# A transformer block on one core: diagonal blocks of a triangular inverse laid out one per partition, keys and queries left unnormalised, attention outputs handled four query tiles at a time

## The chip, the core and the metric

The kernel runs on one core of a Trainium2 chip. The metric is the device time of one execution in microseconds. Three runs of the kernel before took 1466.9 to 1472.14 us; their median is 1470.46 us.

## What is computed

One residual block over 1024 tokens of width 1024: a norm, one projection, two kinds of attention heads, an output projection, and a feed-forward part. The change lies in the heads, of which there are eight forgetting-attention heads ("fox", width 64) and four gated delta-rule heads ("gdn", width 128). Cut to what matters:

```python
# fox head: softmax over the causal prefix with a decay bias, then an RMS norm of the output
logits = q @ k.T * scale + cum[:, None] - cum[None, :]        # masked
o = softmax(logits) @ v;  o = rms_norm(o, fox_out_norm)
# gdn head: q and k are first divided by their norms (rsqrt(sum(x*x) + EPS))
m = strict_lower((k * beta) @ k.T * decay)
t_inv = inverse(eye + m)                                      # unit lower triangular
u = t_inv @ (v * beta);  w = t_inv @ (k * beta * exp(gc))
a = (q @ k.T) * decay
# then a scan over the chunks of tokens
v_new = u_c - w_c @ state
o_c = (q * exp(gc)) @ state + a_c @ v_new
state = state * g_last + k_dec.T @ v_new
```

The kernel uses chunks of 128 tokens (the reference has 64), which is the same function.

## The kernel before

The program has four stages on TensorE: the input projection (`in_up`), the heads, the output projection (L2970 to L2972), and the feed-forward part (`up` and `d_product`). The change is in the heads.

In the heads stage three kinds of work are woven together: the **preparation** of a gdn head, the **scan** over the chunks of the gdn head before it, and the **fox tiles**, 64 of them (8 heads of 8 query tiles). The preparation of head `p` is a list of steps, `HEAD_PREP`. Each step is a *fill*: TensorE writes four 128x128 results into one of three PSUM banks, and VectorE or ScalarE reads the bank (`read`). A fill is either four transposes (`four_turned`, L2722) or four products in float32 (`four_products`, L2717). A name such as `("X", 0, 4)` is step, half of the head (four of its eight chunks) and level. `k`, `q`, `v`, `z` turn the loaded rows; `knT`, `qnT`, `kbT`, `qdT` turn scaled copies back; `N` and `A` are the two score products. The inverse is built by doubling: from blocks of 1 to blocks of 128 in seven levels. Level 0 is `M0`; each level above it is a product `X` (masked on its way out), a product `TX`, and a transposed copy `XR` (a product at the last level). `W` and `U` apply the inverse.

The norm of k and of q goes around four engines: ScalarE squares the bank (`square`), VectorE sums and adds EPS (`norm_mean`), GpSimd raises to the power -0.5 (`norm_power`, L2430), and VectorE scales (`norm_scale`, L1990). Only then can `knT` or `qnT` be turned.

A fox tile is: `scores` on TensorE (L2828 to L2830), a masked row maximum on VectorE (`fox_scores`), the exponential on ScalarE, `turn` (L2846), a copy by VectorE or ScalarE in turn, and `times_v` (the `pv` items, L2860) into a PSUM bank. Then ScalarE copies the 64 output columns out (L1513) and squares them with a sum (L1516), once per tile. After four tiles VectorE forms the mean square (`mean`, L2081 and L2083), GpSimd takes the power (L2485), and VectorE scales the four tiles one at a time (`fox_norm`, L2091).

The order on every engine is fixed when the program is built. `plan_prep`, `plan_scan` and `plan_fox` give each item an engine and a planned time, and `ORDER` is each engine's list sorted by it; the constant `PHASE` is the planned length of a head. An engine takes its list in order: whatever it waits for holds everything behind it. All loads and stores are issued by SyncE, also in a planned order.

## Time and profile before

| | us |
|---|---|
| median of three runs | 1470.46 |
| span of the profiled execution, first to last instruction | 1465.4 |
| TensorE busy in the span | 1379.2 (94%) |
| VectorE, ScalarE, GpSimd busy | 944.7, 658.4, 573.6 |
| heads stage, from the first turn of k in the first head to the end of the last `pv` | 313.3 to 718.4 |

The median lies 5 us above the span; the start and the end of the program lie outside the span. A busy time is the union of an engine's instructions. Matmuls overlap their neighbours, so the time that a matmul costs in a sequence is the distance from its start to the next start, not its listed duration.

### The profile page before, as it was taken

How to read it: one execution, taken by the hardware profiler on the slowest of the kernel's cores; microseconds unless marked ns; L12 is line 12 of the kernel's file. 1: busy time of each engine (PE TensorE's matmuls, PEld its weight loads, DVE VectorE, ACT ScalarE, POOL GpSimd, SP SyncE). 2: the span in 40 equal slices, each digit the busy share in tenths (PEclk: the TensorE clock that was granted, in tenths of full speed). 3: DMA queues.
4: the chain of work that ended last, by engine and by line, in shares of the span. 5: the costliest groups of instructions: out<-in, count | busy, mean ns of one | idle time of the engine just before them, and what ended most of it. 6: DMA issues, size and time to landing. Idle time of an engine off the chain costs nothing.

```text
span 1465.4 us, 20680 instructions
## 1 busy us (share of the span) xinstructions
PE 1379.2 (94%) x7379; PEld 1165.7 (80%) x7379; DVE 944.7 (64%) x1506; ACT 658.4 (45%) x1404; POOL 573.6 (39%) x470
## 2 busy tenths in 40 slices
PE   5999999998989899898899889999999999999997
PEld 4778888877989899797688768888888778888885
DVE  6977777765567665765545799655655584444557
ACT  6654334435455555555433532333233344445453
POOL 3733322314152441614401377665564164442001
PEclk9999999998999999999999999999999999999999
DMA  7143333245113131013222244444442995333533
GB/s 207 47 129 103 115 115 115 88 151 179 30 59 102 49 97 44 16 44 102 87 73 86 85 125 159 158 158 159 158 158 102 329 320 168 94 99 105 202 98 144
DMA packets 135325, 177.88 MB, mean 121 GB/s; under 512 B 10492, under 2 KB 82732, under 8 KB 135224
## 3 DMA queue, kind: packets, MB, share of 16 engines
q1 hardware_dynamic: 135224, 176.56, 37.5%
q8 instruction: 60, 0.98, 0.3%
q14 instruction: 41, 0.34, 0.1%
HBM read 124.05 MB, written 52.48 MB: 120 GB/s over the span
## 4 chain that ended last, share of the span: by engine, by line
PE 76%; DVE 10%; issue 5%; POOL 4%; ACT 2%; DMA 2%; SPq 1%; DVEq 0%; POOLq 0%; ACTq 0%
PE ps L2717 7%; PE ps L3018 7%; PE ps L3020 7%; PE ps L3019 7%; PE ps L3031 6%; PE ps L3032 6%; PE ps L3033 6%; PE ps L2668 5%; PE ps L2670 5%; PE ps L2669 5%; PE ps L2860 3%; PE ps L2970 2%; PE ps L2972 2%; PE ps L2971 2%; PE ps L2722 2%
## 5 line engine op out<-in xcount | busy, mean ns | idle before, releaser
L3031 PE MATMUL ps<-db_hi,da_hi 128*128 128x512 f32 x448 | 175.3, 391 | 4.1 <-DVE db_lo L2288 4.0
L3032 PE MATMUL ps<-db_lo,da_hi 128*128 128x512 f32 x448 | 174.4, 389 | 0.0
L3033 PE MATMUL ps<-db_hi,da_lo 128*128 128x512 f32 x448 | 174.3, 389 | 0.0
L2286 DVE TENSOR_TENSOR da_lo<-a_raw,da_hi 128x512 fp32r<-128x512 f32 x112 | 85.6, 764 | 121.3 <-ACT da_hi L1756 121.2
L1756 ACT ACTIVATE da_hi<-a_raw 128x512 fp32r<-128x512 f32 x112 | 70.7, 631 | 159.3 <-PE ps L3033 136.9
L3018 PE MATMUL ps<-bt_hi,ring_hi 128*128 128x512 f32 x320 | 127.2, 397 | 5.3 <-DVE ring_lo L2208 5.2
L3020 PE MATMUL ps<-bt_hi,ring_lo 128*128 128x512 f32 x320 | 126.0, 394 | 0.0
L3019 PE MATMUL ps<-bt_lo,ring_hi 128*128 128x512 f32 x320 | 125.4, 392 | 0.0
L2668 PE MATMUL ps<-i_bt_hi,i_ring_hi 128*128 128x512 f32 x280 | 111.0, 396 | 3.2 <-DVE i_ring_lo L1848 1.8
L2670 PE MATMUL ps<-i_bt_hi,i_ring_lo 128*128 128x512 f32 x280 | 110.3, 394 | 0.0
L2669 PE MATMUL ps<-i_bt_lo,i_ring_hi 128*128 128x512 f32 x280 | 110.0, 393 | 0.0
L3031 PEld LDWEIGHTS ps<-db_hi,da_hi 128*128 128x128 f32 x448 | 84.1, 188 | 25.3 <-DVE db_lo L2288 7.9
L3033 PEld LDWEIGHTS ps<-db_hi,da_lo 128*128 128x128 f32 x448 | 84.1, 188 | 17.4
L3032 PEld LDWEIGHTS ps<-db_lo,da_hi 128*128 128x128 f32 x448 | 84.1, 188 | 17.1
L2534 POOL TENSOR_TENSOR o_rs<-o_ms,halves 128x1 f32<-128x1 f32 x24 | 16.5, 687 | 203.7 <-DVE o_ms L2186 92.3
L2477 POOL TENSOR_TENSOR q_lo<-q,q_hi 128x128 fp32r<-128x128 f32 x64 | 30.6, 479 | 165.1 <-ACT q_hi L1492 156.8
L1655 ACT ACTIVATE ring_hi<-s_w 128x512 fp32r<-128x512 f32 x64 | 40.3, 632 | 120.5 <-PE ps L3020 116.8
L2860 PE MATMUL ps<-v_tok,probs_t 128*128 128x64 f32 x576 | 78.1, 273 | 14.8 <-DVE probs_t L2039 12.7
L2288 DVE TENSOR_TENSOR db_lo<-wd,db_hi 128x512 fp32r<-128x512 f32 x112 | 88.7, 792 | 0.0
L2860 PEld LDWEIGHTS ps<-v_tok,probs_t 128*128 128x128 f32 x576 | 72.5, 193 | 19.3 <-DVE probs_t L2039 15.2
L3018 PEld LDWEIGHTS ps<-bt_hi,ring_hi 128*128 128x128 f32 x320 | 60.7, 190 | 18.8 <-DVE ring_lo L2208 5.6
L3020 PEld LDWEIGHTS ps<-bt_hi,ring_lo 128*128 128x128 f32 x320 | 60.5, 189 | 14.2
(367 smaller groups left out, 3655.2 us busy)
## 6 DMA issues: line engine op xcount, KB each, us to landing
a_raw<-act_dram SPq DMA_DIRECT2D x112, 256.0 KB, 2.6
act_dram<-s_act SPq DMA_DIRECT2D x64, 256.0 KB, 2.2
wd<-in_w_down_dram SPq DMA_DIRECT2D x15, 1024.0 KB, 7.7
act_dram<-c SPq DMA_DIRECT2D x48, 256.0 KB, 4.8
w_top<-in_w_up_dram SPq DMA_DIRECT2D x18, 512.0 KB, 4.3
w_bot<-in_w_up_dram SPq DMA_DIRECT2D x16, 512.0 KB, 5.5
i_top<-in_w_in_dram SPq DMA_DIRECT2D x14, 512.0 KB, 4.0
i_bot<-in_w_in_dram SPq DMA_DIRECT2D x14, 512.0 KB, 5.3
```

Of the source, the lines that this page charges most:

```text
L2288: nc.vector.tensor_tensor(db_lo[s][:, :], d_moving(n), db_hi[s][:, :].bitcast(F32), ALU.subtract).then_inc(d_lo_ready, 1)
L2668: nc.tensor.matmul(acc, i_ring_hi[r][:, k, :], b_hi[:, k, :], start=(first and k == 0), stop=False, skip_group_check=True)
L2669: nc.tensor.matmul(acc, i_ring_hi[r][:, k, :], b_lo[:, k, :], start=False, stop=False, skip_group_check=True)
L2670: last = nc.tensor.matmul(acc, i_ring_lo[r][:, k, :], b_hi[:, k, :], start=False, stop=(k == HK - 1), skip_group_check=True)
L2717: last = nc.tensor.matmul(bank(f)[:, i * P:(i + 1) * P], lhs(i), rhs(i), start=True, stop=True)
L2860: last = nc.tensor.matmul(fox_o(i)[:, 0:FOX_DIM], probs_t[n % 2][:, kb - 4 * c, :], v_tok[h % 2][:, kb, hh * FOX_DIM:(hh + 1) * FOX_DIM], ...
L3018: nc.tensor.matmul(acc, ring_hi[r][:, k, :], b_hi[:, k, :], start=(first and k == 0), stop=False, skip_group_check=True)
L3019: nc.tensor.matmul(acc, ring_hi[r][:, k, :], b_lo[:, k, :], start=False, stop=False, skip_group_check=True)
L3020: last = nc.tensor.matmul(acc, ring_lo[r][:, k, :], b_hi[:, k, :], start=False, stop=(k == HK - 1), skip_group_check=True)
L3031: nc.tensor.matmul(acc, da_hi[s][:, cols], db_hi[s][:, :], start=start, stop=False, skip_group_check=True)
L3032: nc.tensor.matmul(acc, da_hi[s][:, cols], db_lo[s][:, :], start=False, stop=False, skip_group_check=True)
L3033: return nc.tensor.matmul(acc, da_lo[s][:, cols], db_hi[s][:, :], start=False, stop=stop, skip_group_check=True)
```

## The change

The change takes levels 0 to 3 of the inverse out of the fills. The 16x16 diagonal blocks of `N` (8 blocks in each of 8 chunks, 64 in all) are written by eight small DMAs to DRAM and read back with one block in each of 64 partitions. VectorE inverts them there with 16 instructions on 64 partitions (`lanes`), the result goes to DRAM, and eight small DMAs put the blocks on the diagonal of `t_low`, from which level 4 starts. `HEAD_PREP` shrinks: the steps `kbT`, `qnT`, `qdT`, `M0`, `X` and `TX` of levels 1 to 3, `XR` of levels 1 and 2 and one mask turn are gone, and six empty places stand ahead of the first `X`. In all 250 fills become 153: 49 turned fills and 48 product fills fewer.

The scales are moved. `kn` is now k times beta over its square sum (reciprocal and product on VectorE, no power), `N` and `A` use k and q as loaded, the root of the sum goes into `vb`, `exp(gc)` for q is one exponential (`g_last_out`) and one GpSimd product (`q_grown`), and q's norm enters through EPS in the output norm.

Fox outputs: the eight tiles of a head share one PSUM bank, 64 columns each. ScalarE copies four tiles at once and squares them in place in PSUM; VectorE sums the squares; two VectorE products scale four tiles. The first `pv` of each group of four waits for `tail_mean` of the group before it; in the kernel before each `pv` waited for the output copy of the tile before in the same bank. `PHASE` goes from 90 to 68.

```diff
 HEAD_PREP = [
+    ("k", 0, 0), ("k", 1, 0), ("q", 0, 0), ("knT", 0, 0), ("q", 1, 0), ("knT", 1, 0), ("N", 0, 0), ("N", 1, 0),
+    ("v", 0, 0), ("A", 0, 0), ("v", 1, 0), ("A", 1, 0), ("z", 0, 0), ("z", 1, 0), None, None, None, None, None, None,
+    ("X", 0, 4), ("XR", 0, 3), ("X", 1, 4), ("XR", 1, 3), ("TX", 0, 4), ("TX", 1, 4),
...
+            def load_lanes(p):
+                for g in range(2):
+                    sp.wait_ge(dve_prep, DVE_PREP[("read", (p, "N", g, 0))])
+                for b in range(NBLOCK):
+                    rows = slice(BLOCK * b, BLOCK * (b + 1))
+                    sp.dma_start(n_dram[NT * b:NT * (b + 1), :, :].rearrange("t k c -> k t c"),
+                                 n_low[rows, :, :, rows].rearrange("k g t c -> k (g t) c")).then_inc(lanes_moved, 16)
+                sp.wait_ge(lanes_moved, lane_moves(p, "blocks"))
+                sp.dma_start(lane_n[0:LANES, :], n_dram.rearrange("l k c -> l (k c)")).then_inc(lanes_moved, 16)
+            def store_lanes(p):
+                sp.wait_ge(lane_step, LANE_OPS * (p + 1))
+                sp.dma_start(t_dram.rearrange("l c k -> l (c k)"), lane_t[0:LANES, :]).then_inc(lanes_moved, 16)
+                sp.wait_ge(lanes_moved, lane_moves(p, "out"))
...
+                for b in range(NBLOCK):
+                    rows = slice(BLOCK * b, BLOCK * (b + 1))
+                    sp.dma_start(t_low[rows, :, :, rows].rearrange("c g t k -> c (g t) k"),
+                                 t_dram[NT * b:NT * (b + 1), :, :].rearrange("t c k -> c t k")).then_inc(lanes_moved, 16)
...
             def norm_scale(name):
+                nc.vector.reciprocal(k_scale[:, g, :], means[:, g, :]).then_inc(scale_step, 1)
...
+                nc.vector.tensor_tensor(k_scale[:, g, :], k_scale[:, g, :], gates_all[:, BETA, p, four], ALU.mult).then_inc(scale_step, 1)
...
+                nc.vector.tensor_tensor(kn[:, g, :, :], bank4(FILL[name] - 1), wide(k_scale[:, g, :], P), ALU.mult).then_inc(dve_prep, 1)
...
+            def lanes(p, part):
...
+                elif part == 2:
+                    dve.wait_ge(lane_step, done + 12)
+                    nc.vector.tensor_tensor(lane(lane_p, 0, (64, 8), (8, 8), (1, 8)), lane(lane_n, 8, (1, 8), (0, 8), (16, 8)),
+                                            lane(lane_t, 0, (0, 8), (1, 8), (16, 8)), ALU.mult).then_inc(lane_step, 1)
+                    dve.wait_ge(lane_step, done + 13)
+                    nc.vector.tensor_reduce(lane(lane_x, 0, (1, 64)), lane(lane_p, 0, (8, 64), (1, 8)), AX_X, ALU.add).then_inc(lane_step, 1)
...
             def fox_out(i):
-                nc.scalar.activation(mixed_fox(qb // HT, h)[:, qb % HT, hh * FOX_DIM:(hh + 1) * FOX_DIM], fox_o(i)[:, 0:FOX_DIM], ACT.Copy)
-                if i >= 1:
-                    act.wait_ge(fox_read, i)
-                nc.scalar.activation(sq_fox[:, :], fox_o(i)[:, 0:FOX_DIM], ACT.Square, accum_out=fox_ss[:, hh, qb:qb + 1]).then_inc(fox_read, 1)
+                nc.scalar.activation(mixed_fox(half, h)[:, :, hh * FOX_DIM:(hh + 1) * FOX_DIM], fox_o4(i // NT, half), ACT.Copy).then_inc(fox_copied, 1)
+                act.wait_ge(fox_copied, i // HT + 1)
+                nc.scalar.activation(fox_o4(i // NT, half), fox_o4(i // NT, half), ACT.Square).then_inc(fox_read, 1)
...
             def mean(tail):
+                dve.wait_ge(fox_read, 2 * n + half + 1)
+                nc.vector.tensor_reduce(fox_ss[:, n % 2, cols], fox_o4(n, half), AX_X, ALU.add).then_inc(rr_ready, 1)
...
             def fox_norm(n, half):
+                nc.vector.tensor_tensor(o, o, wide(fox_ms[:, n % 2, half * HT:(half + 1) * HT], FOX_DIM), ALU.mult).then_inc(fox_scaled, 1)
+                dve.wait_ge(fox_scaled, FOX_NORM[("fox", (n, half))])
+                nc.vector.tensor_tensor(o, o, stacked(fox_norm_row[:, :], HT), ALU.mult).then_inc(mixed_ready, 1)
...
             def prep(name):
                 elif what == "X":
+                    if lev == BASE:
+                        pe.wait_ge(lanes_moved, lane_moves(p, "t_low"))
...
             def times_v(i, c):
                 if c == 0:
-                    if OUT_BEFORE[i] is not None:
-                        pe.wait_ge(fox_read, OUT_BEFORE[i] + 1)
+                    if i >= HT and qb % HT == 0:
+                        pe.wait_ge(tail_mean, MEAN[("fox", (i - HT) // NT, 1 - qb // HT)])
```

The first place is TensorE at the start of the third gdn head, from the first turn of k (`c_raw_k`) on. Other names: `probs` and `probs_t` belong to fox tiles, `u_all`, `a_t`, `kd` to the scan. Before:

```order
L2722 MATMUL ps<-const,c_raw_k 128x128 x4
L2846 MATMUL ps<-const,probs_161 128x128 x3
L2722 MATMUL ps<-const,c_raw_v 128x128 x4
L2860 MATMUL ps<-v_tok_139,probs_t_163 128x64 x3
L2722 MATMUL ps<-const,c_raw_q 128x128 x4
L2898 MATMUL ps<-u_all_151,a_t_147 128x128
L2901 MATMUL ps<-u_all_151,kd_143 128x128
L2722 MATMUL ps<-const,c_raw_v 128x128 x4
```

After:

```order
L2838 MATMUL ps<-const,c_raw_k 128x128 x4
L2953 MATMUL ps<-const,probs_166 128x128 x3
L2838 MATMUL ps<-const,c_raw_k 128x128 x4
L2965 MATMUL ps<-v_tok_144,probs_t_168 128x64 x3
L2838 MATMUL ps<-const,c_raw_q 128x128 x4
L3004 MATMUL ps<-u_all_156,a_t_152 128x128
L3007 MATMUL ps<-u_all_156,kd_148 128x128
L2935 MATMUL ps<-k_split_163,q_hi_170 128x512
L2936 MATMUL ps<-k_split_163,q_lo_172 128x512
```

Both halves of k are now turned ahead of q and v.

The second place is VectorE in the same head, with the instructions on the lanes (`lane_n`, `lane_p`, `lane_t`, `lane_x`) and what stands among them after the change; none of the lane rows stands in the kernel before:

```order
L2152 TENSOR_TENSOR a_t_151<-ps,decay 128x512
L2088 COPY lane_t<-lane_n 64x8
L2090 TENSOR_TENSOR lane_p<-lane_n,lane_t 64x8
L2092 COPY lane_t<-lane_n 64x4x2
L2094 TENSOR_TENSOR lane_t<-lane_p,lane_n 64x4x2
L2097 TENSOR_TENSOR lane_p<-lane_t 64x8
L2100 TENSOR_TENSOR lane_t<-lane_t,lane_p 64x4x2
L2184 TENSOR_TENSOR v_new<-u_all_156,ps 128x128
L2105 TENSOR_TENSOR lane_p<-lane_n,lane_t 64x64 x2
L2108 TENSOR_REDUCE lane_x<-lane_p 64x32
L2111 TENSOR_TENSOR lane_p<-lane_t,lane_x 64x64 x2
L2114 TENSOR_REDUCE lane_t<-lane_p 64x2x4x4
```

The scan's `v_new` and `state` and a fox copy now stand in VectorE's list behind instructions that wait for DMAs.

The third place is TensorE in the same head where `times_v` goes from the fourth to the fifth fox head (`v_tok_144` to `v_tok_143`). Before:

```order
L2860 MATMUL ps<-v_tok_139,probs_t_163 128x64 x4
L2722 MATMUL ps<-const,t_inv 128x128 x4
L2828 MATMUL ps<-k_split_157,q_hi_166 128x256
L2829 MATMUL ps<-k_split_157,q_lo_168 128x256
L2830 MATMUL ps<-causal_bf,ident_bf 128x128
L2860 MATMUL ps<-v_tok_139,probs_t_164 128x64 x4
L2846 MATMUL ps<-const,probs_161 128x128
L2717 MATMUL ps<-t_inv,n_low 128x128 x4
L2717 MATMUL ps<-xb,r_inv 128x128 x4
L2860 MATMUL ps<-v_tok_138,probs_t_163 128x64
```

After:

```order
L2965 MATMUL ps<-v_tok_144,probs_t_168 128x64 x4
L2833 MATMUL ps<-t_low,n_low 128x128 x4
L2935 MATMUL ps<-k_split_162,q_hi_171 128x256
L2936 MATMUL ps<-k_split_162,q_lo_173 128x256
L2937 MATMUL ps<-causal_bf,ident_bf 128x128
L2953 MATMUL ps<-const,probs_166 128x128
L2965 MATMUL ps<-v_tok_144,probs_t_169 128x64 x4
L2838 MATMUL ps<-const,t_low 128x128 x4
L2965 MATMUL ps<-v_tok_143,probs_t_168 128x64
```

Two product fills and a turn between the last `pv` of one fox head and the first of the next have become one turned fill.

## Rows read from the trace of the kernel before

**Rows 1.** The page: busy time of each engine; the chain that ended last, by engine.
```profile
PE 1379.2 (94%) x7379; PEld 1165.7 (80%) x7379; DVE 944.7 (64%) x1506; ACT 658.4 (45%) x1404; POOL 573.6 (39%) x470
...
PE 76%; DVE 10%; issue 5%; POOL 4%; ACT 2%; DMA 2%; SPq 1%; DVEq 0%; POOLq 0%; ACTq 0%
```

**Rows 2.** Windows: four heads and the tail; stretch, length, busy by engine, PEclk, DMA.
```profile
313.27:406.80 93.53, 81.95 (x617) 74.77 (x615) 58.27 (x129) 45.37 (x135) 27.54 (x32) 0.93 0.32 102
406.80:495.78 88.98, 81.82 (x684) 77.15 (x682) 57.56 (x143) 48.99 (x159) 32.08 (x35) 0.98 0.25 72
495.78:583.89 88.11, 81.47 (x677) 76.72 (x676) 58.91 (x142) 47.82 (x150) 31.03 (x34) 0.98 0.25 73
583.89:674.31 90.42, 81.10 (x667) 76.24 (x666) 58.58 (x152) 48.21 (x158) 32.60 (x37) 0.98 0.09 25
674.31:718.41 44.10, 36.25 (x266) 31.47 (x265) 28.30 (x75) 30.39 (x99) 28.86 (x22) 0.96 0.40 108
```

**Rows 3.** Groups of TensorE by shape: the X products and the XR turns.
```profile
L2717 PE MATMUL ps<-t_inv,n_low 128*128 128x128 f32 x384 | 51.3, 278 | 0.0
...
L2722 PE MATMUL ps<-const,t_inv 128*128 128x128 f32 x160 | 23.8, 273 | 0.0
```

**Rows 4.** Timeline of TensorE, third head: start, duration, line, count of records.
```profile
521.32 1.00 PE L2860 MATMUL ps<-v_tok,probs_t 128*128 128x64 f32 x8
522.16 0.61 PE L2722 MATMUL ps<-const,qn 128*128 128x128 f32 x4
522.60 0.39 PE L2875 MATMUL ps<-state,w_all 128*128 128x128 f32 x2
...
538.71 1.06 PE L2717 MATMUL ps<-t_inv,n_low 128*128 128x128 f32 x8
539.60 1.06 PE L2717 MATMUL ps<-xb,r_inv 128*128 128x128 f32 x8
```

**Rows 5.** Waits of TensorE from 305 to 722 us: total, times, longest.
```profile
PE ps L2860 <- DVE probs_t L2039: 12.7, 11, 2.6
PE ps L2722 <- DVE qn L1990: 8.9, 8, 2.3
PE ps L2722 <- DVE kn L1990: 5.9, 5, 1.7
```

**Rows 6.** Groups of GpSimd in the heads: busy, mean ns, idle before.
```profile
L2430 POOL TENSOR_TENSOR powers<-means,minus_half 128x4 f32<-128x4 f32 x16 | 16.6, 1039 | 30.1 <-DVE means L1983 30.0
```

**Rows 7.** Groups of VectorE and ScalarE in the heads, same columns.
```profile
L2027 DVE TENSOR_TENSOR t_inv<-t_inv,ps 128x512 f32<-128x512 f32 x40 | 27.5, 687 | 27.1 <-PE ps L2717 26.9
L2056 DVE TENSOR_TENSOR v_new<-u_all,ps 128x128 f32<-128x128 f32 x28 | 7.9, 282 | 6.7 <-PE ps L2875 6.7
L1981 DVE TENSOR_REDUCE sums<-qn 128x4 f32<-128x512 f32 x8 | 5.5, 683 | 1.4 <-ACT qn L1451 1.3
L2083 DVE TENSOR_TENSOR fox_ms<-fox_ss,fox_rr 128x4 f32<-128x4 f32 x16 | 3.0, 189 | 0.6
...
L1473 ACT ACTIVATE r_inv<-ps 128x512 f32<-128x512 f32 x40 | 23.8, 594 | 23.0 <-PE ps L2722 22.6
L1527 ACT ACTIVATE mixed_half<-ps 128x128 f32<-128x128 f32 x32 | 8.8, 274 | 20.1 <-DVE state L2067 16.6 <-PE ps L2898 2.5 <-DVE state L2064 1.1
```

**Rows 8.** DMA issues: count, KB each, median us to landing.
```profile
act_dram<-s_act SPq DMA_DIRECT2D x64, 256.0 KB, 2.2
c_raw_k<-proj_dram SPq DMA_DIRECT2D x3, 512.0 KB, 3.4
```

**Rows 9.** Timeline of SyncE's queue near the start: start, duration of the issue.
```profile
12.86 2.65 SPq L986 DMA_DIRECT2D gate_w<-in_w_in_dram  x1
...
20.38 0.29 SPq L996 DMA_DIRECT2D row_bias<-in_gdn_dt_bias_dram  x1
20.72 0.31 SPq L997 DMA_DIRECT2D row_a<-in_gdn_a_log_dram  x1
```

**Rows 10.** A window in the fourth head, with the columns of rows 2.
```profile
610.00:615.00 5.00, 5.00 (x31) 4.87 (x31) 1.39 (x5) 1.02 (x4) 1.80 (x2) 0.69 0.28 79
```

## What the trace of the kernel before lets one predict

> **What bounds the kernel now.** I read the page first, then windows, groups of instructions, waits, and the timeline. The page says that TensorE is busy for 94% of the span and makes up 76% of the chain that ended last [rows 1]. The change lies in the heads alone, so the windows count. In them TensorE is busy 81 to 82 us of each head's 88 to 94, and 36 of the 44 us of the tail; VectorE works 58 to 59 us per head, ScalarE 45 to 49, GpSimd 28 to 33 [rows 2]. So TensorE's own work bounds the heads, with some 7 to 12 us of idle per head. Its waits name two things: at the start of a head it waits for the scaled k and q (`kn` 5.9 us, `qn` 8.9 us in all), and `pv` waits for VectorE's copies, 12.7 us in 11 waits [rows 5]. The first kind goes back to GpSimd's power, 1039 ns for four columns and 30 us of waiting for the sums before it [rows 6]; VectorE stands still behind it, which also holds copies.
>
> **The price of a fill.** Listed durations overlap, so I take starts. Two product fills start at 538.71 and 539.60: 0.89 us for four products (eight records, since a float32 product makes two). A turned fill takes from 522.16 to 522.60: 0.44 us. Eight records of `pv` take from 521.32 to 522.16: 0.84 us [rows 4]. The count is checked by the groups: 384 records of X are 48 fills, 160 records of turned `t_inv` are 40 [rows 3].
>
> **1. Fills taken out: -64.3 us.** 48 product fills (X and TX of levels 1 to 3) at 0.89 are 42.7 us; 49 turned ones at 0.44 are 21.6 us. All of it is on the engine that bounds the stage, 16 us of each head's 81.
>
> **2. The trip of the blocks: +27 us.** This is new: between the last `N` and the first `X` the blocks go to DRAM, to VectorE's lanes, to DRAM, and back, and nothing of the head but `v`, `A` and `z` can be done meanwhile. Step by step:
> - VectorE's read of `N`: 0.69 us [rows 7] and a signal, 0.8.
> - Eight small stores. An issue on an idle queue comes 0.34 us after the one before (20.38, 20.72) [rows 9], so the last starts after 2.4. For the landing the nearest row is the smallest transfer with one, 256 KB in 2.2 us; a load of 512 KB takes 3.4 [rows 8]. 8 KB should be no slower than 256: 2.2. Together 4.6.
> - The load with one block per partition: 2.2.
> - 16 VectorE instructions. Six with 8 elements at 0.19, four with 64 and two sums over 128 at 0.28 (the 128x128 form), two products of 512 at 0.69 and two sums of 512 at 0.68 [rows 7]: 1.1 + 1.7 + 2.7 = 5.5. Among them stand four others of the scan and the fox tiles, some 1.9 us. Together 7.4.
> - The store, 2.2, and eight small loads, 4.6.
>
> The sum is 21.8 us. What TensorE has in its list for that time is, in the third head, two products and four turns (3.5), three second and two first halves of scan steps (2.5), 26 turned and 22 `pv` blocks (2.9 + 4.6) and three score sets (2.4): 15.8 us, by the pitches above and those of the same stretch for the rest; in the four heads 10.3, 15.0, 15.8 and 15.5. The first has less because no scan runs beside it. Over the four, 87.2 - 56.6 = 30.6 us are not covered. TensorE would not have run that work without gaps, though: apart from the starts of heads it idles some 6% of a head, 3 us of these. I take 27. Bounds: the landings take 3.4 instead of 2.2 and the lane instructions, which step through memory by 16 or 17 elements, take twice their time: 32 us a trip, +41, together +68. Below, the waits that TensorE has today inside those stretches, and those of point 4, all fall into the trip: +5.
> The Trainium skill, in "DMA: Bandwidth & Descriptors", section "Anatomy of one DMA — SWDGE (gpsimd) path", gives one DMA a fixed cost of about 2.0 us that does not depend on its size, for the GpSimd path; these are issued by SyncE. With 2.0 in place of 2.2 the four landings would make the trip 0.8 us shorter, an estimate of 3 us over the kernel.
>
> **3. The start of a head: -14 us.** k's chain is now square 0.59, sum 0.68, three short ones at 0.19, scale 0.69 [rows 7], 2.5 us and about 3 with the signals, with no GpSimd in it. TensorE's own work between the first k and `knT` is 0.9, 2.9, 3.1 and 4.4 us. So of 14.8 us of waits [rows 5] about 4 stay, and of the copies that waited behind VectorE's stop I count 3 as gone.
>
> **4. Outputs four at a time: +8 us.** What is saved on ScalarE and VectorE is off the path: neither is above 0.7 of a head. The new wait is on it. After the last `pv` of a group follow the copy and the square of 256 columns (between 0.27 for 128 and 0.59 for 512, so 0.38 each), the sum (0.4), and two short ones [rows 7]: 1.9 us with signals. Where a fox head ends and the next begins TensorE has 0 to 1.1 us in between (0.5 on average; the third fence of the order shows 0.44), so 1.4 us are open at seven places, of which one lies inside a trip. Between the halves of one head there are 1.4 to 5.2 us, which cover it. The old wait had a single tile's copy and square behind it and does not appear among the waits. From 0, where other stalls swallow it, to +20, where queues on two engines double it.
>
> **5. Clock: +2 us; the rest: 0.** After a stretch of idle the granted clock falls to its lower level: 610 to 615 us has 0.69 on average [rows 10], 3.1 us at half, a loss of 1.6. Each head has such a drop at its start. I expect one per trip instead, and one more in the first head. The added memsets on GpSimd, the shorter load of constants and the 20 issues per head on SyncE stand before or beside other work: 0, or up to 1 us for the memset ahead of the first fox tile. The tail keeps its 44 us: its fills are none before and after.
>
> **The sum.** -64.3 + 27 - 14 + 8 + 2 = -41.3 us of the span of 1465.4. The median of the runs lies 5 us above the span, for the start and end that the change leaves alone, so 1470.5 - 41 = 1429 us. Per head: the three later ones go from 88 to 90 us to about 76, the first from 93.5 to some 86.
>
> **Rivals.**
> - *The trip is hidden.* TensorE's other waits fall into it: a stalled TensorE lets VectorE and ScalarE get ahead, so that the work behind runs without gaps. For it: the idle of 7 to 12 us per head has that cause. Against it: its list has 15 us of work for 22 us of trip whatever the others do. Then -64.3 - 14 + 8: 1400 us. Chance 0.22.
> - *The trip is long.* Landings of 3.4 us, strided lanes at twice the price, VectorE held at the head of its list so that `v_new` and copies wait too: +41 against the forecast at the bound, half of it likely. 1446 to 1475. Chance 0.17.
> - *Slower: small DMAs issue slowly.* The trip has 16 of them in a row. The third load of `gate_w`, in pieces of 16 bytes, kept the queue for 2.65 us [rows 9]; at that price 16 issues take 37 us longer, the trip 59 us, and the time is 1429 + 4 x 37 = 1577. It decides from a trip of 32 us on, or 0.98 us an issue: then the 41 us are gone. Against it: that load had 1024 pieces and large loads ahead of it, these have 128 each, and the queue is half empty in the heads (DMA share 0.09 to 0.32 [rows 2]). The Trainium skill speaks against the change here: the same page, section "Specifications", has transfers below 512 bytes done as read-modify-write, and these have 64; it gives no price, and no run here shows one. Chance 0.06.
>
> That the change doesn't do what it says is no rival: the lists of instructions show 97 fills fewer.
>
> **How the numbers follow.** The forecast, 1413 to 1446, has 0.55. Faster by over 0.3%, about what a measurement of this kernel can tell from no change, needs 1466 or less: 0.55 + 0.22 + 0.13 of the long trip = 0.90. Within 0.3%: 0.04, all from the long trip. Slower: 0.06. The range has to hold 0.8: from 1397, which takes in most of the hidden trip, to 1458, half of the long one.
>
> **What would show it.** Right: 250 fills become 153; the first `X` of each head waits for the loads of `t_low`, by 6 to 12 us, most in the first head; `kn` and `qn` are gone from TensorE's waits; `pv` waits 1 to 2 us for VectorE's mean at the passes from fox head to fox head; GpSimd and ScalarE busy less; stages outside the heads equal to 1 us. Wrong: lane instructions well above 0.7 us, issues well above 0.34 us, or a wait for `t_low` above 15 us push it up; no wait for `t_low` pulls it to 1400. A tail longer than 46 us would mean that the shared bank costs more than point 4 says.

## The result, and the profile after

The ratio is 0.9911, 95% interval 0.9897 to 0.9926: 13 us faster, not 41. The direction was right, the time lies at the upper edge of the forecast's range, and the gain is a third of the forecast. The profiled execution has a span of 1455.4 us.

The page of the changed kernel, busy times and the chain by engine [rows 1 before]:

```profile
PE 1343.6 (92%) x6800; PEld 1127.0 (77%) x6800; DVE 932.4 (64%) x1506; ACT 626.4 (43%) x1205; POOL 539.1 (37%) x438
...
PE 76%; DVE 12%; issue 3%; DMA 3%; ACT 3%; SPq 2%; POOL 1%; DVEq 0%; ACTq 0%; POOLq 0%
```

TensorE has lost 579 instructions, but only 36 us of busy time where 64 were taken out. The windows say where. I cut each head in three: the **start**, from the first turn of k to the end of VectorE's read of the second `N`; the **trip**, from there to the first `X`; the **rest**, to the next head's first turn. Columns as in [rows 2]; the last line of a group adds it up. First the starts and trips of the changed kernel, then the four rests, then the tail.

```profile
313.61:340.26 26.65, 18.63 (x99) 15.47 (x97) 17.96 (x41) 14.51 (x37) 11.75 (x11) 0.81 0.60 198
...
488.82:509.95 21.13, 14.71 (x88) 13.12 (x88) 17.78 (x38) 11.89 (x32) 11.01 (x10) 0.76 0.08 25
...
sum 86.84, PE 62.68 PEld 54.20 DVE 66.10 ACT 47.91 POOL 44.67; mean PE 15.67 PEld 13.55 DVE 16.52 ACT 11.98 POOL 11.17
...
419.24:446.12 26.88, 18.03 (x126) 16.02 (x125) 16.38 (x49) 9.88 (x32) 6.60 (x8) 0.76 0.60 167
509.95:534.30 24.35, 20.38 (x131) 18.18 (x130) 14.48 (x41) 9.27 (x27) 4.25 (x5) 0.79 0.42 122
...
sum 98.36, PE 70.35 PEld 62.28 DVE 62.19 ACT 35.91 POOL 19.19; mean PE 17.59 PEld 15.57 DVE 15.55 ACT 8.98 POOL 4.80
...
sum 157.42, PE 151.15 PEld 142.85 DVE 93.85 ACT 76.59 POOL 24.72; mean PE 37.79 PEld 35.71 DVE 23.46 ACT 19.15 POOL 6.18
...
656.23:707.16 50.93, 40.76 (x265) 35.66 (x264) 27.21 (x73) 28.15 (x72) 28.45 (x21) 0.83 0.34 94
```

The rests are full (151 of 157 us busy, clock 0.94 to 1.00). The starts are 62.7 busy of 86.8, the trips 70.4 of 98.4, and in both the granted clock is 0.74 to 0.90 where a whole head of before had 0.93 to 0.98 [rows 2]. The tail has 50.9 us for 44.1 and a clock of 0.83.

TensorE's waits from 305 to 722 us [rows 5 before]:

```profile
PE ps L2965 <- DVE probs_t L2167: 14.7, 14, 5.0
PE ps L2838 <- DVE kbg L2075: 7.3, 4, 3.7
PE ps L2965 <- DVE fox_ms L2212: 7.0, 4, 3.9
PE ps L2833 <- DMA t_low<-t_dram: 6.8, 2, 3.7
...
PE ps L2965 <- issue: 5.6, 3, 3.4
```

`kn` and `qn` are gone, as forecast. In their place stand `kbg` (a fill bank that VectorE has not finished with), the mean of the fox outputs (`fox_ms`), and the blocks from DRAM (`t_low`). The three waits called `issue` are the mean's too: at each of them VectorE's mean had ended 0.1 us before the `pv` began. So `pv` waits for the mean 12.6 us in seven places, which are the seven passes from one fox head to the next.

### The profile page after: what moved, and what is told of

Read it like the earlier page. It is cut to its first block, busy times and chain, and to the rows that moved or that the text cites. A ratio compares the mean times of both kernels' runs of the same rounds, so it can differ in the third digit from the quotient of the medians.

```text
span 1455.4 us, 19172 instructions
## 1 busy us (share of the span) xinstructions
PE 1343.6 (92%) x6800; PEld 1127.0 (77%) x6800; DVE 932.4 (64%) x1506; ACT 626.4 (43%) x1205; POOL 539.1 (37%) x438
## 4 chain that ended last, share of the span: by engine, by line
PE 76%; DVE 12%; issue 3%; DMA 3%; ACT 3%; SPq 2%; POOL 1%; DVEq 0%; ACTq 0%; POOLq 0%
PE ps L3124 7%; PE ps L3126 7%; PE ps L3125 7%; PE ps L3137 6%; PE ps L3139 6%; PE ps L3138 6%; PE ps L2784 5%; PE ps L2786 5%; PE ps L2785 5%; PE ps L2833 5%; PE ps L2965 3%; PE ps L3076 2%; PE ps L3078 2%; PE ps L3077 2%; PE ps L2953 1%
## 5 line engine op out<-in xcount | busy, mean ns | idle before, releaser
L1824 ACT ACTIVATE da_hi<-a_raw 128x512 fp32r<-128x512 f32 x112 | 70.7, 631 | 159.7 <-PE ps L3139 140.0
L2965 PE MATMUL ps<-v_tok,probs_t 128*128 128x64 f32 x576 | 87.9, 295 | 31.2 <-DVE probs_t L2167 14.7
L2965 PEld LDWEIGHTS ps<-v_tok,probs_t 128*128 128x128 f32 x576 | 81.1, 213 | 39.3 <-DVE probs_t L2167 19.3
L3138 PEld LDWEIGHTS ps<-db_lo,da_hi 128*128 128x128 f32 x448 | 84.2, 188 | 17.1
```

The costliest lines, as they stand in the source:

```text
L2965: last = nc.tensor.matmul(fox_o(i), probs_t[n % 2][:, kb - 4 * c, :], v_tok[h % 2][:, kb, hh * FOX_DIM:(hh + 1) * FOX_DIM], start=(kb == 0 ...
L3138: nc.tensor.matmul(acc, da_hi[s][:, cols], db_lo[s][:, :], start=False, stop=False, skip_group_check=True)
```

## Taking the change apart

In this part "after" is 1457.3 us. The kernel before ran beside each group of runs at 1470.1 to 1471.7. Idle is length less TensorE's busy time; time at half clock is 2 x (1 - PEclk) x length. Windows come from one execution of each kernel, whose time lies up to 5 us from the median of its runs, so a difference of 2 or 3 us between windows of two kernels says little by itself.

**no_trip: the trip left out.** The gather, the lane instructions and the scatter leave the plan; `t_low` is filled once, with identity blocks, and the first `X` waits for that alone. The kernel then inverts another matrix, in the same number of fills.

```diff
-            at("sp", t + 1.5, "gather", h)
-            for part in range(LANE_PARTS):
-                at("dve", t + 7.0 + 1.8 * part, "lane", h, part)
-            at("sp", t + 14.5, "scatter", h)
...
-                        pe.wait_ge(lanes_moved, lane_moves(p, "t_low"))
+                        pe.wait_ge(cleared, 10)
```

> The changed kernel without the trip of the blocks: the eight stores, the load, the 16 lane instructions, the store and the eight loads are left out, and t_low holds identity blocks from the start (so the inverse is of another matrix; all fills stay). In the trace of the changed kernel the four stretches from the last N to the first X are 98 us long, and TensorE's list there is 57 us by the pitches of the prediction. Theory A, the trip is the largest loss: TensorE's idle and the lower clock of these stretches go, about 42 us, of which a few come back as waits elsewhere: 1415 to 1430 us. Theory B, the trip is covered by other work and the loss lies at the head starts: under 15 us gained, 1443 or more.

Measured: 1421.3 us, 36.0 less than after. The four trips, second and fourth and the sum:

```profile
406.06:425.14 19.08, 16.66 (x125) 15.46 (x125) 9.64 (x32) 7.94 (x27) 5.59 (x7) 0.88 0.80 209
...
564.74:582.51 17.77, 15.43 (x123) 13.90 (x121) 11.11 (x29) 9.91 (x28) 5.80 (x6) 1.00 0.19 51
sum 66.74, PE 57.90 PEld 52.80 DVE 39.17 ACT 33.86 POOL 18.52; mean PE 14.47 PEld 13.20 DVE 9.79 ACT 8.46 POOL 4.63
```

The same work takes 66.7 us here and 98.4 with the trip: 31.6 of the 36.0 lie inside the trips. Another 3 lie behind them, where the clock is still down. Theory A.

**old_outs: the fox outputs as before.** One tile at a time, with the waits of before.

```diff
-        if qb % HT == HT - 1:
-            at("act", v + 0.7, "out", i)
+        at("act", v + 0.7, "out", i)
...
-                    if i >= HT and qb % HT == 0:
-                        pe.wait_ge(tail_mean, MEAN[("fox", (i - HT) // NT, 1 - qb // HT)])
+                    if OUT_BEFORE[i] is not None:
+                        pe.wait_ge(fox_read, OUT_BEFORE[i] + 1)
```

> The changed kernel with the fox outputs of before: one tile at a time, copied and squared by ScalarE with a sum, four scalings of one tile by VectorE, two banks in the tail; everything else as after. Theory A, the outputs taken four at a time cost more than the 8 us predicted, because the first pv of a group waits until VectorE comes to the mean (7.0 us in 4 waits, with a fall of the clock behind) and because the tail has grown from 44 to 50 us: 12 to 16 us faster than after, 1441 to 1445. Theory B, what they save on ScalarE and VectorE outweighs the wait: 0 to 8 us slower than after, 1457 to 1465.

Measured: 1446.6 us, 10.6 less than after, just outside theory A's interval and far from theory B. The tail is 47.1 us instead of 50.9.

**sq_sbuf: the wait for the mean alone.** ScalarE squares the copy in SBUF instead of PSUM in place, so the bank is free after the copy.

```diff
-                        pe.wait_ge(tail_mean, MEAN[("fox", (i - HT) // NT, 1 - qb // HT)])
+                        pe.wait_ge(fox_copied, i // HT)
```

> The changed kernel with the squares of four fox tiles taken from the copy in SBUF and written to SBUF, so that the first pv of the next group waits for ScalarE's copy alone and no longer for VectorE's mean. Theory A, the wait for the mean (7.5 us in five places, 3.9 the longest) is a real loss, and so is the clock that falls behind it: 5 to 9 us faster than after, 1448 to 1452. Theory B, the next wait takes its place: within 3 us of after.

Measured: 1451.4 us, 5.9 less: theory A. The wait itself stands in the timeline of the changed kernel at the start of its fourth head (start, duration, engine, line): ScalarE's square, VectorE's list, and the `pv` on TensorE. The square ended at 580.60 (580.23 + 0.37):

```profile
580.23 0.37 ACT L1584 ACTIVATE ps<-ps 128x256 f32<-128x256 f32 x1
...
581.02 0.69 DVE L2066 TENSOR_TENSOR kn<-ps,k_scale 128x512 f32<-128x512 f32 x1
581.63 0.68 DVE L2075 TENSOR_TENSOR kbg<-ps,gates_all 128x512 f32<-128x512 f32 x1
582.23 0.68 DVE L2053 TENSOR_REDUCE q_sums<-q_sq 128x4 f32<-128x512 f32 x1
...
583.28 0.42 DVE L2209 TENSOR_REDUCE fox_ss<-ps 128x4 f32<-128x256 f32 x1
...
584.12 0.66 PE L2965 MATMUL ps<-v_tok,probs_t 128*128 128x64 f32 x2 [3.90 <-DVE fox_ms L2212]
```

The sum of squares comes 2.7 us after its input was there, because k's and q's norms stand ahead of it on VectorE, and TensorE stood for 3.9 us.

**old_outs_no_trip: both.** The edits of no_trip and old_outs together.

> Both at once: the fox outputs of before, and the trip of the blocks left out (t_low holds identity blocks, so the inverse is of another matrix). What is left of the change is the 97 fills fewer and the new start of a head. The trip alone was worth 36.0 us, the outputs 10.7. Theory A, the two costs are separate and the start of a head gives nothing back: they add up, 1409 to 1414 us, some 4 us more than the fills' 64 us alone would leave of the 1470 of before. Theory B, they are in part the same idle: 1416 to 1421. Theory C, the 14 us that the prediction gave to the head starts are there and were hidden by one of the two: 1392 to 1402.

Measured: 1406.6 us, between theories A and C, nearer A. Without the trip the outputs cost 14.7 (1421.3 to 1406.6), without the new outputs the trip costs 40.0 (1446.6 to 1406.6); either way the two together cost 50.7. The four heads of this run, and its longest waits:

```profile
sum 295.94, PE 261.74 PEld 240.71 DVE 196.44 ACT 170.78 POOL 89.61; mean PE 65.44 PEld 60.18 DVE 49.11 ACT 42.70 POOL 22.40
```

```profile
PE ps L2842 <- DVE kbg L2080: 8.8, 5, 3.7
PE ps L2971 <- DVE probs_t L2172: 7.9, 12, 2.3
PE ps L2957 <- ACT probs L1574: 6.8, 2, 3.9
...
PE ps L2866 <- DVE kbg L2080: 1.5, 1, 1.5
```

This is the row that settles most. TensorE's busy time in the four heads fell by 64.6 us (before, the four heads of [rows 2] add up to 326.3 busy in 361.0), as step 1 has it for the fills. The idle time is 34.2 us; before it was 34.7. So the new head starts gave **nothing** to the stage. The starts by themselves, first in the kernel before (where they hold more fills) and then in this run:

```profile
sum 138.36, PE 111.92 PEld 100.25 DVE 94.33 ACT 81.32 POOL 80.28; mean PE 27.98 PEld 25.06 DVE 23.58 ACT 20.33 POOL 20.07
...
sum 84.23, PE 60.56 PEld 51.92 DVE 66.11 ACT 50.12 POOL 45.46; mean PE 15.14 PEld 12.98 DVE 16.53 ACT 12.53 POOL 11.37
```

Idle fell there from 26.4 to 23.7 us, not by 14, and what follows in the heads has 10.5 idle for 8.3.

## Why the head starts gave nothing

**kb_act: `kbg` of heads 2 to 4 on ScalarE**, in four pieces, ahead of VectorE's `kn`.

```diff
-                at("dve", t + 3.0, "kb", name)
+                at("act" if h else "dve", t + (1.3 if h else 3.0), "kb", name)
```

> The changed kernel with the product kbg (k times exp(g)) of heads 2 to 4 made by ScalarE in four pieces of 128 columns, ahead of VectorE's kn, instead of by VectorE behind it. Theory A, the start of a head is bound by VectorE's list, and TensorE waits for the bank that kbg holds (9.1 us of waits in all, 5 of them in heads 2 to 4) with the clock down behind it: 5 to 10 us faster than after, 1447 to 1452. Theory B, ScalarE's square, four pieces and VectorE's wait for them are as long: within 3 us of after.

Measured: 1456.8 us, theory B in the time. The starts came out shorter, 83.9 us for 86.8, the trips and rests 3.2 longer.

**qd_late: GpSimd's product for q at the second `N`.**

```diff
-            at("pool", t + (7.0 if h == 0 else 6.0), "qd", h)
...
             at("sp", t + 1.5, "gather", h)
+            at("pool", t + 0.5, "qd", h)
```

> The changed kernel with GpSimd's product for q (128x1024, 2.4 us) moved from the start of a head to the time of the second N. In the changed kernel small instructions of VectorE at the head starts take several times their usual length while GpSimd runs its two 128x1024 products: the addition of EPS for q 0.49 and 1.2 us where 0.17 is usual, one scaled gdn tile 1.36 where 0.35 is usual. Theory A, these stretched instructions lie on the chain of the head start: the four starts get 1 to 2 us shorter each, 1450 to 1454. Theory B, VectorE has slack around them, or the stretched instructions move to another place: within 3 us of after.

Measured: 1456.7 us, theory B again: starts 84.9, and what they gave went into rests at a lower clock (161.9 for 157.4). The addition of 1.2 us that the expectation counts for q is k's (L2051).

**starts: all of it at once, without trip and new outputs.** old_outs_no_trip with kb_act and qd_late, and the two turns of q behind `A`.

```diff
-    ("k", 0, 0), ("k", 1, 0), ("q", 0, 0), ("knT", 0, 0), ("q", 1, 0), ("knT", 1, 0), ("N", 0, 0), ("N", 1, 0),
+    ("k", 0, 0), ("k", 1, 0), ("knT", 0, 0), ("knT", 1, 0), ("N", 0, 0), ("N", 1, 0),
-    ("v", 0, 0), ("A", 0, 0), ("v", 1, 0), ("A", 1, 0),
+    ("v", 0, 0), ("A", 0, 0), ("v", 1, 0), ("A", 1, 0), ("q", 0, 0), ("q", 1, 0),
```

> old_outs_no_trip (the fox outputs of before, the trip left out, so the inverse is of another matrix) with VectorE's list at the head start shortened: kbg of heads 2 to 4 on ScalarE, GpSimd's product for q at the second N, and the two turns of q with their squares and sums behind A instead of between k and knT. Without these the four starts, from the first turn of k to VectorE's read of the second N, were 84.2 us long with VectorE busy 66.1. Theory A, VectorE's list and the banks that wait for it bound the start: the starts shrink to 68 to 74 us and the time from 1406.6 to 1392 to 1400. Theory B, the chain from k to N itself or the lower clock bounds it: the starts stay above 80 us, 1403 to 1407.

Measured: 1411.1 us (1405.9 to 1415.9, the profiled one 1405.9): not faster than 1406.6. The sums of its starts and of the stretches from `N` to `X`, and its first wait:

```profile
sum 68.82, PE 47.53 PEld 41.96 DVE 48.62 ACT 49.09 POOL 39.83; mean PE 11.88 PEld 10.49 DVE 12.15 ACT 12.27 POOL 9.96
...
sum 77.31, PE 65.53 PEld 58.42 DVE 51.46 ACT 43.82 POOL 24.56; mean PE 16.38 PEld 14.60 DVE 12.86 ACT 10.95 POOL 6.14
```

```profile
PE ps L2852 <- DVE kn L2081: 10.1, 7, 3.5
```

The starts shrank as theory A has it, from 84.2 to 68.8 us, and the stretches behind them grew from 62.8 to 77.3: together 147.0 and 146.1. `kbg` is gone from the waits, and `kn` is back with 10.1 us. Here a wait that was cured at the start of a head came back further on under another name. That one engine bounds the whole stretch was not shown: VectorE is busy for 100 of the 146 us, TensorE for 113.

## What the trip can and cannot hide

**loads_late: the lanes' store ahead of the next head's loads.**

```diff
-            at("sp", t + 14.5, "scatter", h)
+            at("sp", t + 1.6, "scatter", h)
```

> The changed kernel with the store of the lanes and the eight loads of t_low issued by SyncE ahead of the next head's loads of v, q, g and z (and of the fox loads that stand among them). In the second head of the changed kernel the store of the lanes took 6.5 us behind these loads, in the others 1.9. Theory A, the trip's end sets the time: the second head gains about 4.5 us and the others under 1: 1451 to 1454. Theory B, SyncE now holds the loads back until the lanes are done, and the next head or fox head waits for them: no gain, 1457 or slower.

Measured: 1459.0 us, theory B. The second trip did fall from 26.9 to 23.0 us. Behind it TensorE stood 4.6 us for a `v_new`, because VectorE stood 4.8 us at the next fox head's k (`k_split`), whose load now came after the trip.

**spread20 and spread20b: more fox and scan work inside the trip.** 20 empty places ahead of the first `X` instead of 6; spread20 has the order of loads_late too, spread20b has not.

```diff
-("z", 1, 0), None, None, None, None, None, None,
+("z", 1, 0)] + [None] * 20 + [
-PHASE, LAST_PHASE, FOX_START = 68.0, 34.0, 8.0
+PHASE, LAST_PHASE, FOX_START = 88.7, 34.0, 8.0
```

> The changed kernel with 20 empty places ahead of the first X instead of 6 (the length of a head in the plan grows in proportion, the lanes stand later in VectorE's list, and the lanes' store goes ahead of the loads): by the pitches of the prediction TensorE's list from the last N to the first X grows from 10.0, 13.8, 14.9 and 14.4 us to 14.6, 18.9, 19.9 and 20.3, taken from the stretch behind the first X. Theory A, TensorE's list was too short for the trip: about 5 us per head are covered that were idle, and the time falls by 14 to 22 us, to 1435 to 1443. Theory B, fox tiles cannot run faster there than VectorE and ScalarE let them, and the stretch gets longer with them: within 6 us of after.

Measured: 1479.1 us, outside both theories: a late fox load again (ScalarE waits 13.4 us for `kk_raw`), this time with TensorE idle for 15.1 us in one piece:

```profile
457.83 1.54 PE L2965 MATMUL ps<-v_tok,probs_t 128*128 128x64 f32 x6 [15.13 <-DVE probs_t L2167]
```

> The spreading of fox and scan work into the trip again (20 empty places ahead of the first X, TensorE's list there 14.6, 18.9, 19.9 and 20.3 us in place of 10.0, 13.8, 14.9 and 14.4), now with the loads in SyncE's order as in the changed kernel; spread20 had them behind the store of the lanes, and in its second head TensorE stood 15.1 us for a fox load that came late. Theory A, the list was too short for the trip: 8 to 20 us faster than after, 1437 to 1449. Theory B, fox tiles are bound there by VectorE, ScalarE and the lower clock, so that the trip gets longer by what is put into it: within 5 us of after or slower.

Measured: 1465.0 us, 7.7 slower than after, the time of theory B. Its second and third trip are 37 us long, 10 to 13 more than in the changed kernel, though some 5 us of work were added to each; VectorE is busy for 23 us of them:

```profile
412.85:449.76 36.91, 27.99 (x167) 24.70 (x167) 23.65 (x66) 13.40 (x41) 8.22 (x10) 0.72 0.50 136
504.16:541.42 37.26, 29.74 (x180) 26.56 (x179) 23.27 (x65) 13.07 (x39) 7.13 (x9) 0.77 0.42 121
```

The trips are 40 us longer in all, the starts and rests 29 shorter. But the blocks are not what these trips end on. In heads 2 to 4 the last of them had landed 7.3, 7.8 and 7.5 us before the first `X`: TensorE was still at the work pushed in. So 20 places are too many for this trip, and whether fewer would have gained was not run.

**combo6, and three further steps from it.** combo6 is old_outs, kb_act and qd_late together, with the loads of v, q, g and z behind the lanes' store and the fox loads one tile earlier, so that none comes late.

```diff
-        if qb == 2 and 1 <= n < 2 * GDN_HEADS - 1:
+        if qb == 1 and 1 <= n < 2 * GDN_HEADS - 1:
```

> The fox outputs of before, kbg of heads 2 to 4 on ScalarE, GpSimd's product for q at the second N, the loads of v, q, g and z behind the store of the lanes but the fox loads one tile earlier; the empty places stay at 6. Theory A, the small gains add up once no load comes late: 1434 to 1441. Theory B, what is gained at a start or at a trip's end is lost to a lower clock behind it, as in the single runs: 1443 to 1448, as old_outs alone.

Measured: **1437.3 us**, ratio to the kernel before 0.9768 (0.9748 to 0.9787): theory A, and faster than both kernels. Against old_outs its starts fell from 86.0 to 78.6 us and its trips from 96.3 to 93.7. Alone, kb_act, qd_late and loads_late moved the time by less than 2 us each, and the earlier fox loads were not run alone, so which of them makes the 9.3 us against old_outs is not separated.

> combo6 with 20 empty places in place of 6 and the lanes and their store later in the plan in proportion. Theory A, the trip can take more fox work once its loads are in time: 5 to 15 us faster than combo6, 1422 to 1438. Theory B, the trip gets longer by what is put into it: as combo6 or slower, 1440 to 1455.

Measured for combo20, combo6 with 20 empty places: 1452.0 us, the time of theory B. Here too the blocks were back 7.8, 5.7 and 6.9 us before the first `X` of heads 2 to 4.

> combo6 with the two turns of q, their squares and sums behind A instead of between k and knT. The four starts were 78.6 us long in combo6. Theory A, the start is bound by VectorE's list, and the trip, whose list in turn grows by two fills, has room for them: 5 to 9 us faster than combo6, 1428 to 1433. Theory B, what is gained at the start is lost in the trip: 1434 to 1439.

Measured for combo_q, combo6 with the turns of q behind `A`: 1445.1 us, worse than both theories. The starts fell to 70.7 us and the trips rose to 110.1 (combo6: 93.7); VectorE's busy time in the trips rose from 63.4 to 73.8.

> combo_q with every second one of the eight small stores and of the eight small loads issued by ScalarE in place of SyncE. In the changed kernel eight issues on one queue took 3.6 us, 0.43 to 0.46 each. Theory A, the trip's own length sets the time: 1.8 us less at each end, 3.6 per head, 8 to 14 us faster than combo_q. Theory B, ScalarE's own queue is held up by the issues and by its wait for the lanes, and the copies behind them come later: within 4 us of combo_q or slower.

Measured for combo_q2, with half of the small DMAs issued by ScalarE: 1448.6 us, the time of theory B. From the read of `N` to the landing of the last block the trips did get shorter, by 1.8 to 3.8 us each. But the blocks were then back 2.2 to 8.9 us before the first `X`, which came behind TensorE's own list, so that the shorter trips brought nothing.

## Is the lower clock a loss of its own?

**warm and warm_mm: idle work on TensorE in the waits**, into the bank that the next item overwrites; transposes in warm, products in warm_mm.

```diff
+            def idle_turns(dst, count):
+                for _ in range(count):
+                    nc.tensor.transpose(dst, ident, ident)
```

> The changed kernel with idle transposes of the identity on TensorE, from the first turn of k to the first X of each head: two ahead of each turn of probs, four of half size ahead of most first pv, two ahead of knT and N, eight ahead of the first X, each into the bank that the item itself then overwrites, after the wait for the bank and before the wait for the data. Theory A, the lower clock in these stretches (34 us at half in the head starts, 42 in the trips, 9 behind the trips) is a loss of its own: with TensorE kept busy the half-clock time falls below 40 us and the time by 6 to 12 us, to 1445 to 1451. Theory B, the lower clock only stretches work that would have waited anyway (for VectorE at the starts, for the blocks in the trips): within 4 us of after, or slower by the idle transposes themselves.

Measured: 1466.0 us, slower by the idle work as theory B allows, and the half-clock time of starts and trips stayed where it was, 75.7 us for 76.5. The third trip is busy for 28.0 of 31.1 us, and its clock is 0.67 (first row).

> Run warm with products of the identity (128x128, one for two transposes; 64 columns ahead of pv) in place of the idle transposes, at the same places of the changed kernel. Theory A, TensorE's clock stays up with products where it fell with transposes, and the lower clock is a loss of its own: half-clock time from the first turn of k to the first X below 50 us (76 in the changed kernel and in warm), 1443 to 1453 us. Theory B, the clock rises but nothing is gained, since the starts wait for VectorE and the trips for the blocks whatever the clock: half-clock time below 50 us, 1455 to 1468. Theory C, the clock does not rise either: above 65 us, 1460 to 1468 as warm.

Measured: 1462.7 us; half-clock time 54.0, not below 50 as theory B has it, which otherwise fits. The third trip (second row) now has the full clock.

```profile
510.03:541.11 31.08, 28.00 (x160) 24.50 (x158) 15.43 (x42) 9.49 (x27) 5.12 (x6) 0.67 0.51 144
```

```profile
515.03:538.49 23.46, 19.71 (x159) 17.76 (x157) 15.60 (x41) 9.48 (x27) 5.63 (x6) 1.00 0.42 124
```

With the clock at 1.00 this trip takes 23.5 us, in the changed kernel at 0.79 it took 24.4; all four take 101.9 and 98.4. What ends a trip differs. In the changed kernel the first `X` of the four heads began 0.1, 0.1, 0.8 and 0.8 us after the last block had landed, so that a higher clock had no more than that to bring forward there, as long as the blocks come when they do. In the third trip of warm_mm it was 0.04 us: the blocks end it. In the third trip of warm the blocks were back 6.3 us before the `X`, and TensorE's own list at the lower clock ended it.

> combo6 with the same idle products. combo6 had 24 us at half clock in the starts and 43 in the trips. Theory A, the clock is a loss of its own: 1424 to 1433 us. Theory B, only the clock changes: 1435 to 1442. Theory C, neither changes, the idle products add to TensorE's list: 1440 to 1450.

Measured for combo6_mm, the idle products in combo6: 1446.5 us, the time of theory C, though the half-clock time fell from 67 to 46. Neither run with idle products gained by its higher clock. Since the idle products are also work, it stays open what a higher clock at no cost would give.

More of the change, by code:

```diff
@@ L279, in turn_bank @@
     return 3 if n in LATE_TURNS and n % 2 == 1 else 6
-def out_bank(i):
-    return 2 if i in LATE_TILES and i % 2 == 1 else 7
 TURN_BEFORE = {n: max((m for m in range(n) if turn_bank(m) == turn_bank(n)), default=None) for n in range(NFC)}
-OUT_BEFORE = {i: max((j for j in range(i) if out_bank(j) == out_bank(i)), default=None) for i in range(NFT)}
 def norms_of(t):
-    return max(count for (_, (_, tile)), count in NORM.items() if tile == t)
+    return max(count for (what, (_, part)), count in NORM.items() if part == (t if what == "gdn" else t // HT))
 IN_PRE = 2
@@ L393, in build @@
         FP = FT // 2
-        const = placed("const", 16512, [P, N_CONST - 1, P])
+        const = placed("const", 16512, [P, 2 + LEVELS - 1 - BASE, P])
+        lane_n = placed("lane_n", 18560, [P, BLOCK * BLOCK])
+        lane_t = placed("lane_t", 19584, [P, BLOCK * BLOCK])
+        lane_p = placed("lane_p", 204736, [P, 512])
+        lane_x = placed("lane_x", 147104, [P, 64])
         ident = const[:, IDENT, :]
@@ L2000, in k_beta, with lane @@
                     after(dve, NPAIR - 1, 4)
[L2001 removed]
+                nc.vector.tensor_tensor(kbg[:, g, :, :], bank4(FILL[name] - 1), wide(gates_all[:, G_EXP, p, 4 * g:4 * g + 4], P), ALU.mult).then_inc(dve_prep, 1)
+            def lane(tile, offset, *dims):
+                return bass.AP(tile[:, :].tensor, offset, [[tile.shape[1], LANES]] + [list(d) for d in dims])
@@ L2112, in take @@
                     elif kind == "kb":
-                        k_beta(n)
+                        k_grown(n)
+                    elif kind == "lane":
+                        lanes(n, item[2])
                     elif kind == "read":
@@ L2500, in z_weighted @@
                 nc.gpsimd.tensor_tensor(z_tok[h % 2][:, :, :], z_tok[h % 2][:, :, :], stacked(gdn_norm_row[:, :], NT), ALU.mult).then_inc(z_normed, 1)
+            after(pool, NPAIR - 1, 3)
+            nc.gpsimd.memset(t_low[:, :, :, :], 0.0).then_inc(cleared, 1)
             for item in ORDER["pool"]:
@@ new lines, in prep @@
+                    four_products(f, lambda i: knT[g][:, i, :], lambda i: c_raw["q"][:, tok[i]])
+                elif what == "X":
+                    if lev == BASE:
+                        pe.wait_ge(lanes_moved, lane_moves(p, "t_low"))
+                        below = t_low
+                    else:
+                        after_dve("read", "TX", g, lev - 1)
+                        below = t_inv
+                    four_products(f, lambda i: n_low[:, g, i, :], lambda i: below[:, g, i, :])
```

332 lines of the change are left out of this document (196 added, 136 removed), and 13 rows, old and new, of the table HEAD_PREP.

## The prediction, step by step

| step | predicted | measured |
|---|---|---|
| 1 fills | -64.3 | -64.6 of busy time in the four heads |
| 2 trip | +27 | +36.0; +40.0 beside the old outputs |
| 3 head start | -14 | about 0: idle of the heads 34.7 before, 34.2 without trip and new outputs |
| 4 outputs | +8 | +10.6; +14.7 without the trip |
| 5 clock | +2 | within the rows above |

The terms of steps 2 and 4 go in pairs, 36.0 with 14.7 or 40.0 with 10.6. So of the 27 us that the forecast missed, 14 are step 3, 9 to 13 step 2, and 3 to 7 step 4; the 2 of step 5 are in these.

**Step 1** came out to 0.3 us: here starts, not listed durations, gave the price of a fill.

**Step 3 failed in its mechanism.** It took TensorE's waits for `kn` and `qn` as the price of GpSimd's power and gave back all but 4 us of 14.8. The power was the last link, not the only bound. With it gone VectorE's own list (sums, scale, `kn`, `kbg`) holds the fill banks, and `kbg` waits of 10.3 us (8.8 + 1.5) took the place. VectorE formed a `kbg` in the kernel before too, but from the copy `kn`, and a bank of k was free as soon as it had been scaled. Now `kbg` is read out of the bank itself, behind `kn`, so that the bank is free one VectorE product later; and both halves of k are turned one after the other. The prediction followed k's chain up to `knT` and has no term for the bank. kb_act and starts took `kbg` of heads 2 to 4 off VectorE, and the time did not fall, so `kbg` is not the only bound either: what limits the starts stays open.

**Step 2 had the mechanism, and was too small.** The trip is on the path of every head, as forecast. Each is 23.5 to 26.9 us long where 21.8 was worked out, of which 0.7 is the read of `N` itself that these windows leave out. The sign given for it did not come, a wait of 6 to 12 us for `t_low` in each head: it is 3.1 and 3.7 us in the first two, and none in the others. TensorE's 28.0 us of idle in the trips lie mostly further ahead (10 us of it for VectorE's copies `probs_t`), and it came to the first `X` about when the blocks did. What made it longer: SyncE's queue in the second head, VectorE's long lane products, and the DMA issues of the fourth trip (median to landing):

```profile
419.31 3.63 SPq L1155 DMA_DIRECT2D n_dram<-n_low  x8
424.05 0.45 SPq L1158 DMA_DIRECT2D lane_n<-n_dram  x1
...
434.53 0.47 SPq L1163 DMA_DIRECT2D t_dram<-lane_t  x1
441.06 3.64 SPq L1172 DMA_DIRECT2D t_low<-t_dram  x8
```

```profile
L2124 DVE TENSOR_TENSOR lane_p<-lane_t,lane_x 64x512 f32<-64x512 f32 x4 | 4.3, 1083 | 0.1
L2118 DVE TENSOR_TENSOR lane_p<-lane_n,lane_t 64x512 f32<-64x512 f32 x4 | 4.1, 1020 | 0.0
```

```profile
n_dram<-n_low SPq DMA_DIRECT2D x8, 8.0 KB, 1.5
t_low<-t_dram SPq DMA_DIRECT2D x8, 8.0 KB, 1.7
lane_n<-n_dram SPq DMA_DIRECT2D x1, 64.0 KB, 2.0
t_dram<-lane_t SPq DMA_DIRECT2D x1, 64.0 KB, 1.9
```

Eight issues took 3.6 us, 0.45 each and not 0.34; the landings of the fourth trip were 1.5 to 2.0, a little less than the 2.2 taken, and in the other trips up to 3.0, but for one store in the second head. The Trainium skill, "DMA: Bandwidth & Descriptors", section "Anatomy of one DMA — SWDGE (gpsimd) path", gives a fixed cost of some 2.0 us that does not depend on the size, for the GpSimd path. The landings of the fourth trip, on SyncE's queue, lie near it. The two lane products over 512 elements took 1.02 and 1.08 us, not 0.69, and the lane instructions with what stands among them 8.4 to 9.0 us a trip, not 7.4. In the second head the lanes' store, issued at 434.53, was followed by the loads of `t_low` only at 441.06: 6.5 us, behind the next head's loads. So 84 us (four times 21.8, less the reads of `N`) became 98. Some 3 us more lie behind the trips, where the clock is still down (8.8 us at half in the first two rests), which the prediction had not counted.

**Step 4** named the right wait and its seven places. The forecast had 1.4 us at each of the six outside a trip; they hold 0.5 to 3.9, 9.2 in all, and the one inside a trip 3.4. The step did not count that VectorE comes late to the sum, by 2.7 us where the wait is longest. sq_sbuf shows that taking this wait away is worth 5.9 us. The rest of the 10.6 is not in the step; the tail, which was to keep its 44 us, has 50.9, and 47.1 with the old outputs.

**Step 5** counted one drop of the clock per trip. The four heads have 85 us at half clock, 27 without trip and new outputs, about what before had (24). For the same matmuls TensorE's busy time is 284.2 us instead of 261.7, so 22 of the 47 us that trip and outputs add to the heads show up as longer matmuls and 24 as idle time. Whether these 22 are a loss of their own is not shown. With idle products (warm_mm) the half-clock time fell by 22 us and the time rose by 5, but the products are work too.

**The rivals.** "The trip is long" (1446 to 1475) holds the measured time, and part of its cause: VectorE's lane products at 1.5 times their price and late copies, but not its landings of 3.4 us. "Small DMAs issue slowly" fell at 0.45 us an issue. The Trainium skill, "DMA: Bandwidth & Descriptors", section "Specifications", has transfers below 512 bytes done as read-modify-write. No price of it can be seen in the median landings of 1.5 and 1.7 us for pieces of 64 bytes. No run here has the same transfers in larger pieces. "The trip is hidden" fell with no_trip.

## What to carry to other kernels

When a wait is taken out, look at who stands second on the engine that released it, and count what now has to be read before a buffer is free. Compare idle sums of a whole stage, not the names of waits: here the names at the head starts changed and the sum stayed at 34 us. In this kernel a round trip through DRAM in the middle of a dependent chain cost about its length less the work that was ready beside it. Pushing 20 places of work into it overshot, and the work ended after the blocks were back: measure when the blocks land before you choose how much to push in.

## What had not been expected of the hardware

A four-column addition on VectorE took 1.23 us where 0.17 is usual, and ended as GpSimd's 128x1024 product did (576.76 and 576.73); a 128x128 instruction took 1.36 instead of 0.35 and ended 0.15 us after another such product (587.54 and 587.39). Rows of the fourth head start of the changed kernel:

```profile
575.53 1.23 DVE L2051 TENSOR_SCALAR means<-sums 128x4 f32<-128x4 f32 x1
579.72 0.17 DVE L2051 TENSOR_SCALAR means<-sums 128x4 f32<-128x4 f32 x1
...
586.18 1.36 DVE L2229 SCALAR_TENSOR_TENSOR mixed_half<-mixed_half,gdn_ms,z_tok 128x128 f32<-128x128 f32 x1
```

```profile
574.38 2.35 POOL L2571 TENSOR_TENSOR decay<-decay,const 128x1024 f32<-128x1024 f32 x1 [0.89 <-ACT qdT L1497]
585.02 2.37 POOL L2587 TENSOR_TENSOR qdT<-qdT,c_raw_q 128x1024 f32<-128x1024 f32 x1
```

The Trainium skill, "SBUF — State Buffer", section "SBUF: two separate sides", tells of a pair of ports that VectorE and GpSimd lock against each other for a whole instruction. These ends agree with it. Moving one of the two products away (qd_late) gained no time that could be measured. And TensorE's granted clock was 0.67 on average over a trip in which it was busy for 28 of 31 us, with idle transposes among its work, while it was 1.00 with idle products at the same places (busy for 19.7 of 23.5 us).
